# A gated hybrid block with PEER retrieval: 768 instead of 704 value columns gathered, their sum in PSUM, low parts of the expert weights on GpSimd

## The reference

```python
def peer_layer(x, wq, keys, U, Vt):
    ...
    idx = jnp.take_along_axis(
        cand_idx.reshape(T, PEER_HEADS, PEER_TOPK * PEER_TOPK), pos, axis=-1)
    gate = jax.nn.softmax(best, axis=-1).astype(x.dtype)
    ...
    def blk(args):
        xb, ib, gb = args
        u = U[ib]
        hid = jax.nn.gelu(jnp.einsum('td,thkd->thk', xb, u))
        v = Vt[ib]
        return jnp.einsum('thk,thkd->td', gb * hid, v)
```

## Time and profile before

| | |
|---|---|
| median of 3 runs | 2048.5 us (2045.63 to 2049.28) |
| profiled execution, first to last instruction | 2047.2 us |
| PE / DVE / ACT / POOL busy, share of the span | 70 / 79 / 42 / 49% |
| mean granted TensorE clock | 0.841 |
| HBM traffic | 600 MB, 293 GB/s over the span |
| value stage, first to last low part | 1562.0 to 2030.2 us |

### The profile page before, as it was taken

The page is one execution under the profiler, slowest core; times in us unless marked ns, Lnnn a source line. Parts: engine busy times, 40 slices in busy tenths (PEclk is TensorE's granted clock), DMA queues, the critical chain, the costliest instruction groups (busy, mean ns, idle before and its releaser), DMA issues.

```text
span 2047.2 us, 22565 instructions
## 1 busy us (share of the span) xinstructions
...
## 2 busy tenths in 40 slices
...
PEclk9999999999999999965555555555569999999999
DMA  5555434444555555789999999999965999999996
GB/s 207 185 185 185 157 132 144 142 156 155 195 184 185 187 184 176 277 346 407 418 417 415 419 400 421 414 422 414 421 244 195 389 386 390 398 406 390 390 384 235
DMA packets 151803, 601.81 MB, mean 294 GB/s; under 512 B 14720, under 2 KB 14736, under 8 KB 118288
## 3 DMA queue, kind: packets, MB, share of 16 engines
...
...
HBM read 598.29 MB, written 2.10 MB: 293 GB/s over the span
## 4 chain that ended last, share of the span: by engine, by line
PE 55%; DVE 16%; issue 14%; POOL 7%; DMA 6%; ACT 2%; DVEq 0%; POOLq 0%; SPq 0%; ACTq 0%
PE acc L1715 7%; PE acc L1716 7%; PE acc L1717 7%; DVE slots L1470 6%; POOL slots L537 5%; PE acc L1698 4%; PE acc L1700 4%; PE acc L1701 4%; PE acc L2021 3%; PE scr L2022 3%; PE acc L2022 3%; DMA v_raw<-in_v_dense 3%; PE scr L2021 3%; PE scr L2023 3%; PE acc L2023 3%
## 5 line engine op out<-in xcount | busy, mean ns | idle before, releaser
L951 DVE TENSOR_TENSOR w_lo<-raw,w_hi 128x2048 fp32r<-128x2048 f32 x136 | 314.6, 2314 | 281.8 <-ACT w_hi L606 280.7
L1470 DVE SCALAR_TENSOR_TENSOR slots<-slots,acc 128x2048 f32<-128x2048 f32 x188 | 424.6, 2284 | 44.0 <-DMA slots<-in_peer_u,expert 41.7
L606 ACT ACTIVATE w_hi<-raw 128x2048 fp32r<-128x2048 f32 x136 | 260.1, 1913 | 409.0 <-PE acc L1717 263.3
L560 POOL DMA_INDIRECT starts<-in_v_gather,expert x256 | 365.1, 1426 | 92.9 <-DVE X L1620 77.7
L537 POOL DMA_INDIRECT slots<-in_peer_u,expert x256 | 250.2, 977 | 241.9 <-DVE expert L1442 145.2
L545 POOL TENSOR_TENSOR slots<-slots,N 128x2048 f32<-128x2048 f32 x62 | 280.5, 4524 | 37.2 <-DMA slots<-in_peer_u,expert 37.1
L887 ACT ACTIVATE v_hi<-v_raw 128x1344 fp32r<-128x1344 f32 x128 | 170.5, 1332 | 260.5 <-PE scr L2023 202.7
L800 ACT ACTIVATE slots<-slots 128x2048 f32<-128x2048 f32 x62 | 118.4, 1909 | 341.2 <-POOL slots L545 341.2
L1978 PE MATMUL scr<-hot_a,hot_b 128*128 128x128 f32 x448 | 92.4, 372 | 222.1 <-DVE hot_b L1515 158.4
L1620 DVE SCALAR_TENSOR_TENSOR X<-starts,weight,X 128x704 f32<-128x704 f32 x256 | 241.9, 945 | 0.7 <-DMA starts<-in_v_gather,expert 0.3
L1715 PE MATMUL acc<-w_hi,hT_hi 128*128 128x512 f32 x576 | 227.9, 396 | 2.5 <-DVE w_lo L951 2.5
...
## 6 DMA issues: line engine op xcount, KB each, us to landing
...
v_raw<-in_v_dense SPq DMA_DIRECT2D x128, 672.0 KB, 7.4
...
slots<-in_peer_u,expert POOLq DMA_INDIRECT x256, 9.6
starts<-in_v_gather,expert POOLq DMA_INDIRECT x256, 8.0
```

Of the source, the lines that this page charges most:

```text
L560: pool.indirect_dma_start(starts[j][:, :], None, v_gather[:, :], bass.IndirectOffsetOnAxis(ap=expert[:, s // NSEL, s % NSEL:s % NSEL + 1], ...
L606: a.activation(w_hi[:, m % 2, :, :], raw[:, m % 2, :, :], ACT.Copy).then_inc(hi_ready, 1)
L951: v.tensor_tensor(w_lo[:, m % 2, :, :], raw[:, m % 2, :, :], w_hi[:, m % 2, :, :].bitcast(fp32), ALU.subtract).then_inc(lo_ready, 1)
L1470: v.scalar_tensor_tensor(out=slots[j][:, :], in0=slots[j][:, :], scalar=1.0, in1=row, op0=ALU.mult, op1=ALU.mult, accum_out=hid_sum[:, t, ...
```

## The change

Four edits. The column split moves: 768 gathered, 1280 dense, so VBANKS becomes 512, 512 and 256. The sum of the gathered rows is kept in PSUM (`value_sum`, in banks 3 and 4) rather than in X: the first addition of a token tile reads X, the last one writes X, the 126 between read and write PSUM. To make room, the dense sums lie in banks 0 to 2 and 5 to 7, and scatter uses bank 4 in place of bank 5 in the second tile. Third, `low_e` goes from DVE to POOL, between gathers: by `low_at(n)` ahead of gather 2n + 4 while that is below 70, and ahead of gather 2n + 11 after that (at most 255). The SBUF places of the buffers shift with the widths. The host lays out V to the new split. Left out of the diff are those places, the same replacement of `acc`/`scr` by `sums` at the end, and a renaming in an earlier part.

```diff
-CW = 704
+CW = 768
 DW = D - CW
...
+def low_at(n):
+
+    s = 2 * n + 4
+    return s if s < WIDE_FROM else min(2 * n + 11, NT * NSEL - 1)
+
+
+def low_before(s):
+
+    return [n for n in range(BLOCKS) if low_at(n) == s]
...
-        acc = ctx.enter_context(nc.psum_tensor("acc", [P, 2, 2 * GW], fp32))
-        scr = ctx.enter_context(nc.psum_tensor("scr", [P, 2, 2 * GW], fp32))
+        banks = ctx.enter_context(nc.psum_tensor("banks", [P, 8 * GW], fp32))
+        acc = banks[:, 0:4 * GW].rearrange("p (a n) -> p a n", a=2)
+        scr = banks[:, 4 * GW:8 * GW].rearrange("p (a n) -> p a n", a=2)
+        sums = [banks[:, 0:DW], banks[:, 5 * GW:5 * GW + DW]]
+        value_sum = banks[:, 3 * GW:3 * GW + CW]
         vbank = scr[:, 1, 0:GW]
-        scatter_bank = [scr[:, 0, GW:2 * GW], scr[:, 1, GW:2 * GW], vbank, acc[:, 1, GW:2 * GW]]
+        first_bank = [scr[:, 0, GW:2 * GW], scr[:, 1, GW:2 * GW]]
+        scatter_bank = [scr[:, 0, 0:GW], scr[:, 1, GW:2 * GW], vbank, acc[:, 1, GW:2 * GW]]
...
+            def low_e(pair, t):
+
+                pool.wait_ge(e_hi_ready, 2 * pair + t + 1)
+                q, at0 = 2 * pair // (P // PIECES), 2 * pair % (P // PIECES)
+                g.tensor_tensor(e_lo[:, pair % 2, t, :],
+                                weight_of[t][q][:, at0:at0 + 2, :].rearrange("p a s -> p (a s)"),
+                                e_hi[:, pair % 2, t, :].bitcast(fp32), ALU.subtract).then_inc(e_ready, 1)
...
                 if s == STARTS_AHEAD:
                     pool.wait_ge(scattered, 2 + NT * P // SC)
+                    low_e(0, 0)
+                    low_e(0, 1)
                 if s == WIDE_FROM + CRING:
                     pool.wait_ge(e_ready, P // PIECES)
+                for n in low_before(s):
+                    for pair, t in weights_at(n):
+                        low_e(pair, t)
                 gather_value(s)
...
-            def low_e(pair, t):
-
-                dve.wait_ge(e_hi_ready, 2 * pair + t + 1)
-                q, at0 = 2 * pair // (P // PIECES), 2 * pair % (P // PIECES)
-                v.tensor_tensor(e_lo[:, pair % 2, t, :],
-                                weight_of[t][q][:, at0:at0 + 2, :].rearrange("p a s -> p (a s)"),
-                                e_hi[:, pair % 2, t, :].bitcast(fp32), ALU.subtract).then_inc(e_ready, 1)
-
             def add_start(s):
 
                 t, k = s // NSEL, s % NSEL
                 dve.wait_ge(start_landed[start_at(s)], 16 * (len(starts_before(s)) + 1))
                 if s:
                     dve.wait_ge(x_added, s)
-                v.scalar_tensor_tensor(out=X[:, t, 0:CW], in0=starts[start_at(s)][:, :], scalar=weight[:, t, k:k + 1],
-                                       in1=X[:, t, 0:CW], op0=ALU.mult, op1=ALU.add).then_inc(x_added, 1)
+                else:
+                    dve.wait_ge(scattered, 2 + NT * BATCHES)
+                v.scalar_tensor_tensor(out=value_sum if k < NSEL - 1 else X[:, t, 0:CW], in0=starts[start_at(s)][:, :],
+                                       scalar=weight[:, t, k:k + 1], in1=value_sum if k else X[:, t, 0:CW],
+                                       op0=ALU.mult, op1=ALU.add).then_inc(x_added, 1)
...
                 v.tensor_tensor(v_lo[n % 2][:, :], v_raw[n % RAWS][:, :], v_hi[:, n % 2, :].bitcast(fp32),
                                 ALU.subtract).then_inc(v_ready, 2)
-                if n == 0:
-                    low_e(0, 0)
-                    low_e(0, 1)
                 add_start(2 * n)
-                for pair, t in weights_at(n):
-                    low_e(pair, t)
                 add_start(2 * n + 1)
...
-                flat = (acc, scr)[t][:, :, :].rearrange("p a n -> p (a n)")
                 for at0, end in pieces:
-                    last = t_.matmul(flat[:, at0:end], ident[:, :], X[:, t, CW + at0:CW + end], start=True, stop=False,
+                    last = t_.matmul(sums[t][:, at0:end], ident[:, :], X[:, t, CW + at0:CW + end], start=True, stop=False,
...
-                    flat = (acc, scr)[t][:, :, :].rearrange("p a n -> p (a n)")
                     eh, el = e_hi[:, n // 2 % 2, t, e_cols], e_lo[:, n // 2 % 2, t, e_cols]
                     for at0, end in pieces:
-                        to, cols = flat[:, at0:end], slice(at0, end)
+                        to, cols = sums[t][:, at0:end], slice(at0, end)
```

More of the change, by code:

```diff
@@ L275, in build @@
                      [weight_of1[:, q * P // PIECES:(q + 1) * P // PIECES, :] for q in range(PIECES)]]
-        v_raw = [at(f"v_raw{n}", kib, [DW]) for n, kib in enumerate((112, 117.25, 2.75))]
+        v_raw = [at(f"v_raw{n}", kib, [DW]) for n, kib in enumerate((112, 117, 3))]
         v_hi = at("v_hi", 184, [2, DW], f32r)
-        v_lo = [at(f"v_lo{n}", kib, [DW], f32r) for n, kib in enumerate((160, 10.75))]
+        v_lo = [at(f"v_lo{n}", kib, [DW], f32r) for n, kib in enumerate((160, 11))]
         e_hi, e_lo = at("e_hi", 97, [2, NT, 2 * P], f32r), at("e_lo", 101, [2, NT, 2 * P], f32r)
@@ L506, in _ @@
                 size = 2 << lv
-                e_lo, e_up = halves(level[lv % 2], size)
+                part_lo, part_up = halves(level[lv % 2], size)
                 b_lo, b_up = halves(b_tile if lv == LEVELS - 1 else b_chunk, size)
                 ref = b_lo[:, :, size // 2 - 1:size // 2].to_broadcast([P, 8 * S // size, size // 2])
-                g.tensor_tensor(e_lo, ref, b_lo, ALU.subtract)
+                g.tensor_tensor(part_lo, ref, b_lo, ALU.subtract)
                 if lv < LEVELS - 2:
-                    last = g.tensor_tensor(e_up, b_up, ref, ALU.subtract)
+                    last = g.tensor_tensor(part_up, b_up, ref, ALU.subtract)
                 else:
-                    last = g.tensor_copy(e_up, b_up)
+                    last = g.tensor_copy(part_up, b_up)
                 last.then_inc(diff_ready, 1)
@@ L924, in _ @@
                 act.wait_ge(v_used, 2 * BLOCKS - 1 + t)
-                a.activation(junk, y[t][:, 0:DW], ACT.Square, accum_out=stat[:, 5, NT + t:NT + t + 1]
+                a.activation(junk, sums[t], ACT.Square, accum_out=stat[:, 5, NT + t:NT + t + 1]
                              ).then_inc(squared, 1)
```

14 lines of the change are left out of this document (6 added, 8 removed).

## The result

The changed kernel takes **2065.2 us** (median of 4 runs, 2060.9 to 2070.2), the kernel before 2047.1 on the same chip. The ratio of their times is 1.0083, 95% interval 1.0069 to 1.0097 (the two medians alone give 1.0088). It is slower by 0.8%, where 2042.5 was forecast. The profiled execution took 2061.4 us, its span 2059.7; it is near the fast end of its runs, and 12.5 us above the span of before.

What follows compares the result with a forecast made beforehand. PE bounds the value stage now, DMA close behind; after the change the DMA queues at 402 GB/s. Terms -1.9, -10.3, +2, +3, +1 sum to -6 us: span 2041, median 2042.5 us, range 2028 to 2062.

Steps and rivals of the forecast that it cites:

- gathers too late in the ring of seven: Rival, blocks 1 to 33: gathers land after their 6.3 us lead; +27 us (2069.5) or +11 (2053.5); chance 0.17.
- with three it should shrink: Argument against late gathers: the 8 us landing is mostly queueing of four gathers in flight, so three should land sooner.
- the rival's own formula: Late gathers, blocks 1 to 33: period is (landing + 0.9)/2, so 8.0 us gives 4.45 us a block.
- the term of -1.9: First 33 periods of the value stage at 3.60 us instead of 3.658: -1.9 us.
- POOL's spare time: GpSimd in the value stage: cycle closes for periods over 3.35 us; it keeps up if low_e is under 0.89.
- The handover: Blocks 33 and 34, low_e behind nine gathers: PE stands about 5 us; +3 us, bounds 0 and 5.
- Start and end: Value stage: gather 4 behind two low_e at the start, +2 us; last gather behind low_e of block 126, +1.
- The bound of the wide ring: Later 94 periods: DMA queues at 402 GB/s set 3.587 us a block instead of 3.697, -10.3 us.
- The rival of 389 GB/s: Value stage: queues give only what they give now, period 3.706 us; +2.5 with +6, 2057 us; chance 0.15.
- PE-bound: Rival, value stage: PE stays the bound, queues carry 413 GB/s, period 3.51 us; -22.5 with +6, 2032 us; chance 0.15.
- PE and DVE: Value stage paces per block: PE 3.49 us, 0.15 off; DVE 3.39 us, staying under PE.
- that saves POOL little: Value stage: a PSUM addition no longer holds gather issues, but gains POOL little because v_lo held it; no size given.

Runs made afterwards that it cites:

- e10: Changed kernel with the low part of block n ahead of gather 2n+6 from first block to last: 2044.5 us, ratio 0.9974 to the kernel before.
- e6: Changed kernel with the gathered rows' sum back in X, 768 columns and low_e on GpSimd kept: 2098.9 us, ratio 1.0234 to the kernel before.
- e1: Kernel before (704 gathered columns, sum in X) with only low_e moved to GpSimd, placed as in the change: 2099.2 us, ratio 1.0238.
- e3: Changed kernel with v_lo computed by scalar_tensor_tensor instead of tensor_tensor: 2066.9 us, ratio 1.0083 to the kernel before.
- e12: Kernel before (704 gathered columns, sum in X) with low_e on GpSimd, ahead of gather 2n+6: 2078.1 us, ratio 1.0136.

## Why the prediction was wrong

- **The step that failed** is in the rival "gathers too late in the ring of seven", at its "against": "with three it should shrink". The lead of 6.3 us and the limit there were worked out rightly (the lowest tenth had 6.2), and the rival got 0.17. Landings did shrink, from 8.0 to 6.6 us in the median (4.9 to 8.9), but stayed above the limit, and by the rival's own formula 6.6 us give (6.6 + 0.9)/2 = 3.75 us a block, where 3.60 was put into the sum. It took 4.12. The rest, 0.37, was not taken apart; the formula has no place for gathers and low parts that start inside `v_lo` (14 of 38 gathers between 1580 and 1660 us took over 1.1 us), nor for the fact that nothing wins the lost time back. In the sum the term of -1.9 was +15.4.
- **POOL's spare time** was worked out as a closed cycle of 3.35 us, and "POOL keeps up, if `low_e` is under 0.89". `low_e` took 0.75 where nothing held it (0.65 forecast), so by that all was well; in the ring of seven it took 1.13 on the mean. The cycle supposed that GpSimd waits for `e_hi` each time and so falls in a fixed place behind `v_lo`. The trace has four such waits in the whole stage. GpSimd ran free and met `v_lo` at changing places.
- **The handover** was the right mechanism, mis-sized in both terms. The stand was 7.9 us, not 5. Addition 69 was put 2 us behind the end of `v_lo` 34 and ended 3.3 behind it, because its own gather landed 8.0 us after issue and VectorE stood 1.3 us for it, so the first error fed this one. And the stand was counted from the end of that `v_lo`, while PE was through with block 33 when it started, 1.5 us earlier. In the sum 9.1 us were lost, not 3. "The queues idle for some of it only" was true, they moved 367 GB/s; but seven gathers of that went into the lead of the wide ring, and late blocks run no faster for it (3.56 in e10 with half that lead).
- **Start and end**: the second addition of block 2 stood 2 us for its gather, as taken; the end cost 0.4 instead of 1.
- **The bound of the wide ring** was right: 3.600 against 3.587, queues at 403 to 405 GB/s against 402, ACT's wait behind the dense load (150.7) above that behind PE (131.3). The rival of 389 GB/s is out, and PE-bound too: e10 reaches 404 GB/s and 3.56. The ceiling of 435 GB/s that the Trainium skill gives ("DMA: Bandwidth & Descriptors", Where 436 GB/s comes from) was not reached in any slice of these profiles.
- **PE and DVE**: 512 columns every 0.23 us and 256 every 0.12, as taken. The addition took 1.018 (1.01 forecast), so PSUM costs it next to nothing. ("0.96 a ns" does not come out of 1344 in 1.557, which is 0.86; but `v_lo` did get 0.066 us shorter, as taken.) That a PSUM addition does not hold GpSimd was right, and undervalued: "that saves POOL little". With low parts on GpSimd it is worth 34 us of the stage (e6). The rule of the Trainium skill, "SBUF — State Buffer" (Who interferes with whom), of a lock between a DVE instruction with two SBUF inputs and a GpSimd one, agrees with e1, e3, e6 and e12: a low part holds an addition in X and not one in PSUM (1.02 us either way), and an addition in X or a `v_lo` holds a gather that starts behind it. A gather that is being issued did not hold an addition (0.945 us beside one, 0.944 without, before).
